# Forgetting attention's outputs as products of split parts, and a new order of the vector work in the long convolution

## The reference

```python
def forgetting_attention(q, k, v, log_f):      # first block, 8 heads of 64
    ...
        logits = jnp.einsum('bqhd,bkhd->bhqk', qi, k).astype(jnp.float32) * scale
        logits = logits + jnp.transpose(Fi, (0, 2, 1))[..., None] - Fk
        mask = pi[:, None] >= kpos[None, :]
        logits = jnp.where(mask, logits, -jnp.inf)
        w = jax.nn.softmax(logits, axis=-1)
        return jnp.einsum('bhqk,bkhd->bqhd', w.astype(v.dtype), v)

def long_conv(u, k_spec, bias):                # second block, called twice
    L = u.shape[1]
    uf = u.astype(jnp.float32)
    y = jnp.fft.irfft(jnp.fft.rfft(uf, n=2 * L, axis=1) * k_spec[None], n=2 * L, axis=1)[:, :L]
    return (y + uf * bias.astype(jnp.float32)).astype(u.dtype)
```

## Time and profile before

| what | value |
|---|---|
| runs | 1761.53 us median of 3 (1761.25 to 1762.07) |
| the profiled execution's own time | 1761.41 us |
| its span, first to last instruction | 1759.6 us |
| mean granted TensorE clock | 0.999 of full speed |
| PE busy | 1734.5 us (99%) |
| DVE busy | 1038.3 us (59%) |
| ACT busy | 632.1 us (36%) |
| POOL busy | 716.0 us (41%) |

### The profile page before, as it was taken

The page is one execution under the profiler, slowest core; times in us unless marked ns, Lnnn a source line. Parts: engine busy times, 40 slices in busy tenths (PEclk is TensorE's granted clock), DMA queues, the critical chain, the costliest instruction groups (busy, mean ns, idle before and its releaser), DMA issues.

```text
span 1759.6 us, 21355 instructions
## 1 busy us (share of the span) xinstructions
PE 1734.5 (99%) x7750; PEld 1400.3 (80%) x7750; DVE 1038.3 (59%) x1185; ACT 632.1 (36%) x876; POOL 716.0 (41%) x299
## 2 busy tenths in 40 slices
PE   8999999999999999999999999999999999999999
PEld 6887788888788888888788788887877777787887
DVE  6767367766654356457674557785534753958541
ACT  5222222225554656221322222213445644333321
POOL 2443344444422421344344344444355434444443
PEclk9999999999999999999999999999999999999999
DMA  4333233324211221243323233322342014232243
GB/s 171 109 105 102 75 99 101 110 90 168 84 61 59 85 72 37 73 133 99 123 96 111 81 101 100 102 96 90 117 150 72 25 37 167 84 101 92 96 137 114
DMA packets 44830, 172.61 MB, mean 98 GB/s; under 512 B 5033, under 2 KB 5161, under 8 KB 43980
## 3 DMA queue, kind: packets, MB, share of 16 engines
q1 hardware_dynamic: 39312, 150.23, 26.0%
q10 hardware_dynamic: 5436, 21.20, 3.4%
HBM read 160.79 MB, written 10.62 MB: 97 GB/s over the span
## 4 chain that ended last, share of the span: by engine, by line
issue 64%; POOL 17%; PE 16%; POOLq 1%; DVE 1%; ACT 1%; DMA 0%; SPq 0%; DVEq 0%; ACTq 0%
POOL wlo L263 17%; PE psum L297 5%; PE psum L299 4%; PE psum L298 4%; PE psum L1598 1%; PE psum L1587 1%; POOLq L271 0%; DMA raw<-wk_dram 0%; PE psum L1559 0%; ACT whi L285 0%; PE psum L1550 0%; POOLq L261 0%; DVE merged_hi L1277 0%; PE psum L1489 0%; DVE sum L1275 0%
## 5 line engine op out<-in xcount | busy, mean ns | idle before, releaser
L263 POOL TENSOR_TENSOR wlo<-raw,whi 128x1024 fp32r<-128x1024 f32 (+2 forms) x262 | 674.0, 2573 | 995.8 <-ACT whi L285 995.8
L285 ACT ACTIVATE whi<-raw 128x1024 fp32r<-128x1024 f32 (+2 forms) x263 | 290.3, 1104 | 741.4 <-PE psum L299 735.4
L297 PE MATMUL psum<-h_hi,whi 128*128 128x512 f32 x1360 | 539.2, 396 | 7.1 <-POOL wlo L263 3.9
L299 PE MATMUL psum<-h_hi,wlo 128*128 128x512 f32 x1360 | 530.7, 390 | 0.0
L298 PE MATMUL psum<-h_lo,whi 128*128 128x512 f32 x1360 | 530.3, 390 | 0.0
L297 PEld LDWEIGHTS psum<-h_hi,whi 128*128 128x128 f32 x1360 | 256.1, 188 | 68.4 <-issue 9.6
L298 PEld LDWEIGHTS psum<-h_lo,whi 128*128 128x128 f32 x1360 | 256.0, 188 | 54.6 <-issue 3.1
L299 PEld LDWEIGHTS psum<-h_hi,wlo 128*128 128x128 f32 x1360 | 255.8, 188 | 54.3
L297 PE MATMUL psum<-mid_hi,whi 128*128 128x512 f32 x352 | 138.1, 392 | 0.0
L298 PE MATMUL psum<-mid_lo,whi 128*128 128x512 f32 x352 | 137.0, 389 | 0.0
L299 PE MATMUL psum<-mid_hi,wlo 128*128 128x512 f32 x352 | 137.0, 389 | 0.0
(11 more groups left out here) (353 smaller groups left out, 2413.7 us busy)
## 6 DMA issues: line engine op xcount, KB each, us to landing
raw<-wk_dram SPq DMA_DIRECT2D x224, 512.0 KB, 3.7
raw<-wd_dram SPq DMA_DIRECT2D x32, 704.0 KB, 4.1
raw<-wp_dram SPq DMA_DIRECT2D x8, 640.0 KB, 3.9
spectra_scratch<-spec_out ACTq DMA_DIRECT2D x8, 512.0 KB, 6.9
x_scratch<-xT ACTq DMA_DIRECT2D x2, 2048.0 KB, 7.6
xT<-x_scratch ACTq DMA_DIRECT2D x8, 512.0 KB, 4.6
spec<-spectra_scratch ACTq DMA_DIRECT2D x2, 2048.0 KB, 10.1
xT<-x_dram SPq DMA_DIRECT2D x4, 512.0 KB, 7.9
```

Source lines behind the costliest of these rows:

```text
L263: pool.tensor_tensor(wlo[s][:, 0:w], raw[s][:, 0:w], whi[s][:, 0:w].bitcast(F32), ALU.subtract).then_inc(lo_ready, 1)
L285: act.activation(whi[s][:, 0:w], raw[s][:, 0:w], ACT.Copy).then_inc(hi_ready, 1)
L297: pe.matmul(dst, s_hi, m_hi, start=start and i == 0, stop=False, **kw)
L299: last = pe.matmul(dst, s_lo, m_hi, start=False, stop=stop and i == n - 1, **kw)
```

## The change

**Forgetting attention.** The values are kept as pairs `v_pairs`: for each head 128 columns, the 64 of one part and the 64 of the other (hi and lo; which comes first depends on the head's parity). The turned probabilities are split as well (`probT_hi` by ACT, `probT_lo` by DVE, `vector_turned`). `tensor_out` is now two fp32r products per tile, both with the same 128 columns of `v_pairs`, one with `probT_hi` and one with `probT_lo`. The 128 output rows hold the hi part's sum in the head's own rows and the lo part's sum in the other 64. ACT copies the other rows across to `ya_shift`, and POOL adds them to `ya_lo` (`pool_outputs`). The sign of the maximum is taken in the reduction itself (`negate=True`), so the instruction of line 778 goes. `vector_norm` and the copies are put in a new order.

**Long convolution.** In the second half the `vector_part` moves ahead of the sums (`low`), the 8 products and 4 sums are written as product, product, sum, and `x2z` moves from behind `vector_z` to the middle of the next products (j = 0) or behind the last `vector_part` (j = 1).

```diff
+        ya_shift = at(24, "ya_shift", [P, 4, T])
-        v32 = at(88, "v32", [P, TT, T])
+        v_pairs = [at(88, "v_pairs0", [P, 2, 2 * T], F32R),
+                   nc.alloc_sbuf_tensor_at("v_pairs1", [P, 2, 2 * T], F32R, offset=scratch0)]
...
             def tensor_turn(self, pe, h, s):
...
                 if n >= 2:
-                    pe.wait_ge((self.copied0, self.copied1)[s % 2], n // 2)
+                    pe.wait_ge(self.lo, n - 1)
...
             def tensor_out(self, pe, h, s):
-                pe.wait_ge((self.copied0, self.copied1)[s % 2], 2 * h + s // 2 + 1)
+                pe.wait_ge(self.lo, TT * h + s + 1)
                 if s == 0:
                     if h:
                         pe.wait_ge(self.out, h)
+                        pe.wait_ge(self.out_hi, 2 * h)
...
-                pe.matmul(psum[:, 512 * 6 + s * P:512 * 7], v32[:, s, (h // 2) * P:(h // 2 + 1) * P],
-                          probT[s % 2][:, s * P:T], start=s == 0, stop=s == TT - 1).then_inc(self.summed, 1)
+                both = v_pairs[s // 2][:, s % 2, h * P:(h + 1) * P]
+                for i, part in enumerate((probT_hi, probT_lo)):
+                    last = pe.matmul(psum[:, 512 * 6 + s * P:512 * 7], both, part[s % 2][:, s * P:T],
+                                     start=s == 0 and i == 0, stop=s == TT - 1 and i == 1)
+                last.then_inc(self.summed, 1)
...
             def scalar_outputs(self, act, h):
-                for s in range(TT):
-                    self.copy_transpose(act, h, s)
-                    if s and h + 1 < HEADS:
-                        self.scalar_exp(act, h + 1, s - 1)
...
+                self.copy_transpose(act, h, 0)
+                self.copy_transpose(act, h, 1)
                 if h + 1 < HEADS:
-                    self.scalar_exp(act, h + 1, TT - 1)
+                    for t in range(TT):
+                        self.scalar_exp(act, h + 1, t)
+                else:
+                    split_hi_to(act, BASE["sb_q"] + 3)
+                self.copy_transpose(act, h, 2)
+                self.copy_transpose(act, h, 3)
...
                 act.activation(ya_hi[rows, h // 2, :], bank(6)[rows, :], ACT.Copy).then_inc(self.out_hi, 1)
+                if h >= 4:
+                    act.wait_ge(self.ready, h - 3)
+                act.activation(ya_shift[rows, h % 4, :], bank(6)[other[h % 2], :],
+                               ACT.Copy).then_inc(self.out_hi, 1)
...
+            def vector_turned(self, dve, h, s):
+                n = TT * h + s
+                dve.wait_ge((self.copied0, self.copied1)[s % 2], n // 2 + 1)
+                src = psum[:, 512 * (4 + s % 2) + s * P:512 * (5 + s % 2)]
+                dve.tensor_tensor(probT_lo[s % 2][:, s * P:T], src, probT_hi[s % 2][:, s * P:T].bitcast(F32),
+                                  ALU.subtract).then_inc(self.lo, 1)
...
+            def pool_outputs(self, pool, h):
+                rows = main[h % 2]
+                pool.wait_ge(self.out_hi, 2 * h + 2)
+                pool.wait_ge(self.out, h + 1)
+                pool.tensor_tensor(ya_lo[rows, h // 2, :], ya_lo[rows, h // 2, :].bitcast(F32),
+                                   ya_shift[rows, h % 4, :], ALU.add).then_inc(self.ready, 1)
...
-                for t, b in ((1, 6), (2, 4), (3, 5)):
-                    act.activation(v32[:, t, :], bank(b), ACT.Copy).then_inc(self.v, 1)
+                act.wait_ge(self.ready, 32)
+                for t, b in ((0, 7), (2, 4), (3, 5), (1, 6)):
+                    act.activation(self.value_part(t, 0), self.heads(bank(b)), ACT.Copy).then_inc(self.v, 1)
...
+                    if j:
+                        merge2.vector_part(dve, 2 * o, 4 * o + 2)
                     for i in range(2):
                         dve.tensor_tensor(low[i][:, :], high[i][:, :], bank(b + 2 * i + 1), ALU.add).then_inc(self.halves, 1)
...
+                        for i in range(2):
+                            self.vector_products(dve, k_low, low, lower, 2 * i, 2 * i + 2)
+                            self.vector_sums(dve, lower, 8 * n, i, i + 1)
+                        hyena_in.vector_x2z(dve, n - 1)
...
+                        for i in range(2):
+                            self.vector_products(dve, k_high, high, upper, 2 * i, 2 * i + 2)
+                            self.vector_sums(dve, upper, 8 * n + 4, i, i + 1)
...
                 merge2.vector_part(dve, 2 * o + 1, self.forth(1))
+                hyena_in.vector_x2z(dve, 2 * o + 1)
```

More of the change, by code:

```diff
@@ L158, in build @@
         probT = [at(104 + 2 * i, f"probT{i}", [P, T]) for i in range(2)]
+        probT_hi = [at(104 + 2 * i, f"probT_hi{i}", [P, T], F32R) for i in range(2)]
+        probT_lo = [nc.alloc_sbuf_tensor_at(f"probT_lo{i}", [P, T], F32R, offset=scratch0 + (8 + 2 * i) * 1024)
+                    for i in range(2)]
         sq_hi = at(32, "sq_hi", [P, HEADS, T], F32R)
@@ L728, in scalar_exp @@
             def scalar_exp(self, act, h, t):
[L729 to L732 removed]
+                if t == 0 and h >= 2:
+                    act.wait_ge(self.turned, TT * (h - 1))
+                act.wait_ge(self.maxed, TT * h + t + 1)
                 n = (t + 1) * P
@@ L794, in vector, with vector_norm @@
                         self.vector_maximum(dve, h + 1)
-                self.vector_outputs(dve, HEADS - 1)
+                    self.vector_turned(dve, h, 0)
+                    self.vector_turned(dve, h, 1)
+                    if h + 1 < HEADS:
+                        self.vector_norm(dve, h + 1)
+                    self.vector_turned(dve, h, 2)
+                    self.vector_turned(dve, h, 3)
+                self.vector_outputs(dve, HEADS - 1)
+            def vector_norm(self, dve, h):
+                total, inverse = self.cols(h, 1), self.cols(h, 2)
+                dve.wait_ge(self.exped, TT * (h + 1))
+                dve.reciprocal(inverse, total).then_inc(self.inv, 1)
+                dve.wait_ge(self.inv, h + 1)
+                for t in range(TT):
+                    row = self.prob[h % 2][:, t, 0:(t + 1) * P]
+                    dve.tensor_scalar(row, row, inverse[:, t:t + 1], None, ALU.mult).then_inc(self.normed, 1)
@@ new lines, in pool @@
+            def pool(self, pool):
+                u = BASE["gate1"] + 3
+                for h in range(HEADS - 1):
+                    pool.wait_ge(lo_ready, u + h)
+                    self.pool_outputs(pool, h)
+                    pool.wait_ge(self.ready, h + 1)
+                    stream_lo(pool, u + h, u + h + 1)
+                stream_lo(pool, u + 7, u + 9)
+                pool.wait_ge(lo_ready, u + 9)
+                self.pool_outputs(pool, HEADS - 1)
+                pool.wait_ge(self.ready, HEADS)
@@ L944, in vector, with vector_values, heads, value_part @@
                 dve.wait_ge(unit_done, BASE["fox_v"] + 4)
-                dve.tensor_copy(v32[:, 0, :], bank(7)).then_inc(merge1.seven_read, 1)
+                self.vector_values(dve, 0, 1)
+            def vector_values(self, dve, first, last):
+                for i, (t, b) in list(enumerate(((0, 7), (2, 4), (3, 5), (1, 6))))[first:last]:
+                    dve.wait_ge(self.v, i + 1)
+                    dve.tensor_tensor(self.value_part(t, 1), self.heads(bank(b)), self.value_part(t, 0).bitcast(F32),
+                                      ALU.subtract).then_inc(merge1.seven_read if b == 7 else self.cleared, 1)
+            def heads(self, b):
+                return b.rearrange("p (a e c) -> p a e c", e=2, c=HD)
+            def value_part(self, t, lo):
+                v = v_pairs[t // 2][:, t % 2, :].rearrange("p (a e c) -> p a e c", e=4, c=HD)
+                return v[:, :, 1:3, :] if lo else v[:, :, 0:4:3, :]
             def vector_logits(self, dve):
@@ L1326, in tensor_part @@
                 else:
-                    pe.wait_ge(fox.out, HEADS)
+                    pe.wait_ge(fox.ready, HEADS)
                     pe.wait_ge(self.seven_read, 10 + b)
@@ L2302, in build @@
         class LongConvolution:
-            signals = [sem(f"long_{x}") for x in ("even", "halves", "products", "upper_products", "spectrum", "f32",
+            signals = [sem(f"long_{x}") for x in ("even", "halves", "products", "spectrum", "f32",
                                                   "hi", "ready", "back", "gated", "gated_hi", "out")]
@@ L2317, in __init__ @@
                 self.o = o
-                (self.even, self.halves, self.prod, self.upper_prod, self.y, self.f32, self.hi, self.ready, self.back,
+                (self.even, self.halves, self.prod, self.y, self.f32, self.hi, self.ready, self.back,
                  self.out32, self.out_hi, self.out) = LongConvolution.signals
```

87 lines of the change are left out of this document (42 added, 45 removed).

## The result

| what | before | after |
|---|---|---|
| median of the runs | 1761.6 us (1761.25 to 1762.07, 4 runs) | 1747.47 us (1746.88 to 1747.85, 4 runs) |
| ratio, 95% interval | | 0.992, 0.9909 to 0.9932 |
| span of the profiled execution | 1759.6 us | 1745.0 us |

The change saves 14.1 us, 0.8%.

The account below looks back on a forecast made before the run. PE, busy 1734.5 of 1759.6 us, was taken to bound the kernel. Output products 6.0, less 0.15 behind the last head, plus long convolutions 3.1 made 9.0 us saved: 1752.5 us, range 1750.8 to 1756.8.

Parts of the forecast that it names:

- output products: Forgetting attention: two fp32r products replace each float32 one, net 0.75 us less a head, 6.0 us for 8 heads.
- long convolution: Second half: PE's wait for `vector_part` goes and its wait for POOL's low part shrinks, 3.1 us for two convolutions.
- POOL gets in at a pause of DVE: Long convolution: POOL's low part enters only when DVE pauses, forecast behind the third pause; 1.57 us saved for both waits.
- My upper bound: Output products: 0.81 us less a head, 6.5 us in all, if no switch of format costs anything.
- Work beside PE: Forgetting attention: work added on ACT, DVE and POOL stays hidden behind PE's filler halves, costed at nothing.
- Rivals C and D: C: late `probT_lo` chain, 1757 to 1759 us, chance 0.08; D: POOL holds DVE ahead of scalings, up to 1773 us, 0.04.
- Behind the last head: After forgetting attention: ACT's extra copy delays POOL's low part, 0.15 us lost, bounds 0 and 0.7.
- rival A: Long convolutions: POOL gets in at once, a gain of 4.0 us there, 1751.6 us in all, chance 0.13.
- `x2z` of the second half: Long convolution: it would stand for most of POOL's 2.40 us low part, outputs about 3 us late, nothing lost for PE.
- Rival B: Long convolutions: POOL stands as long as now, the wait only moves, no gain there, 1755.7 us, chance 0.13.

Follow-up runs that it names:

- Experiment 2: Two edits of the kernel before, on the feed-forward layer's gain: `e5_pool_behind_mid_lo`, 1759.54 us, and `e7_before_padded`, 1758.82 us.
- e13_early_pause: `e1_fox_only` with the fifth product of the long convolution's second half waiting for the fourth, a pause of 0.1 us: 1750.20 us, ratio 0.9934.
- e3_part_moved_only: `e1_fox_only` with `vector_part` moved ahead of the `low` sums, products, sums and `x2z` in the old order: 1747.17 us, ratio 0.9921.
- e1_fox_only: The changed kernel with the long convolution's vector work put back in the old order, so forgetting attention's edit alone: 1752.43 us, ratio 0.9949.
- e7_before_padded: The kernel before with 28 tiny memsets on DVE behind the last output of forgetting attention: 1758.82 us, ratio 0.9984.
- e15_two_more_products: `e1_fox_only` with two more products ahead of the sums in the second half of each long convolution: 1756.89 us, ratio 0.9970.
- e5_pool_behind_mid_lo: The kernel before with POOL's low part of unit 127 waiting until DVE's `mid_lo` in the second feed-forward layer is done: 1759.54 us, ratio 0.9988.

## Why the prediction was wrong, point by point

Three steps failed: the feed-forward layer was left out (2.7 us), the output products were mis-sized (6.0 us for 7.3), and the long convolution was priced by a rule, POOL gets in at a pause of DVE, that is too strict (3.1 us for 4.6).

**What bounds the kernel.** Right: work off PE counted by itself, and all else mattered only where PE waited.

**Output products (-6.0 forecast, -7.3 found).** The mechanism was right, and the term was mis-sized by 0.18 us a head. Out 0 gave 0.40 as forecast (0.86 to 506.93 - 506.47 = 0.46). Out 1 with its step between formats gave 0.21 as forecast (0.67 to 0.46; the 0.26 from 507.07 to 507.33 shows the 0.09). What I left out is the other side of that step: the two transposes between out 0 and out 1 take 0.14 (506.93 to 507.07) where they took 0.22. Outs 2 and 3 gave 0.17 (0.57 to 0.40) instead of 0.14, and scores and filler together 0.07. My upper bound, 6.5 us, assumed that no step could get cheaper.

**Work beside PE.** Right, all of it at nothing: counted from the head's first score (501.22), the first two `probT_lo` were done at +4.2 (forecast 4.4), PE wanted them at +5.3; the exponentials ended at +5.4 (6.0), the scalings at +6.9 (7.5), the last `probT_lo` at +7.5 (8.2). POOL's low part ended at +5.4 (5.3), 0.2 us ahead of the scalings. Rivals C and D did not come. **Behind the last head** 0.2 us were lost against 0.15.

**The feed-forward layer (nothing forecast, -2.7 found).** This step was missing altogether, so that it stood in the sum at nothing, without a reason. The waits of PE in the kernel before named it, 2.1 us in one place; the prediction passed over it and looked only at the stages that the change touches. Experiment 2 shows that 28 more instructions of DVE ahead of it are enough to win it. What stops DVE for 0.35 us is not shown. That it hangs on the place in DVE's stream is, as far as one padding can show it: the work around that place was the same, and PE's weight loads between the first 15 us and it kept their distance from those of the kernel before to 0.1 us. That it was luck for the change is shown with it.

**Long convolution (-3.1 forecast, -4.6 found).** The step that failed is "POOL gets in at a pause of DVE". I read it from one row in which POOL stood through four sums. In the first convolution after the change POOL did get in at a pause, but at the second pause and not, as forecast, at the third: its request came 3.20 us behind the first product, where 3.40 had been placed, just ahead of that pause and not behind it (rival A's "it misses one by 0.2 us"). In the second convolution it missed the pause and was let in 0.33 us later, without one. The experiments show a different rule: POOL is let in behind the instruction of DVE that runs as it asks, pause or not, when DVE has made few instructions since its last pause, and only at a pause when it has made many. POOL got in behind the fourth (`e13_early_pause`) and the eighth (`e3_part_moved_only`, counted from the first difference, ahead of which DVE pauses), and did not behind the twelfth (the kernel before, `e1_fox_only` and its variants). Where between eight and twelve the limit lies was not tried. Nor was it told apart whether all instructions count or only those that read two tiles in SBUF (the sixth product in `e3_part_moved_only`, the eighth in `e1_fox_only`), or whether it is the time since the pause and not the number (POOL asked 1.9 and 4.4 us behind it where it got in, 6.8 us where it did not). With that, rival A's mechanism was the right one, POOL let in at once, and so was its sign, an instruction of POOL of about 2.5 us (2.39 and 2.73). Its 4.0 us were too small as well, by about 0.14 us a wait. Most of that is a cost of the step behind the wait: in the kernel before the product that had waited at 1538.72 was followed in 0.34 us and not in 0.23, and I had counted only the step ahead of it.
The Trainium skill (SBUF — State Buffer, section Who interferes with whom) says that whoever issues first gets the shared pair for its whole instruction. The prediction took it that the loser then waits for one instruction, which the section does not say. The 0.35 and 0.50 us of the short runs agree with that reading; the 2.7 and 3.9 us of the long ones do not, and the measurement decides.
My expectation that `x2z` of the second half would stand 2 us did not come: it asked together with POOL and won. Rival B did not come.

**The sum.** -7.3 + 0.2 - 2.7 - 4.6 = -14.4 us of the 14.6 of span. Of this 11.7 us belong to the change's two ideas, and one of its three edits in the convolution, `vector_part` ahead of the sums, is enough for its part. With the feed-forward layer left out, the time would have been some 1750 us, just below my range, because two terms erred to the same side.

## What to carry to other kernels

Look at every wait of PE in the profile, also far from the change: a collision of DVE and POOL that is decided by less than 0.2 us can flip with any edit that adds instructions ahead of it, and a few idle instructions in the old kernel tell such a gain from one that the change earned. In these runs, where DVE and POOL held each other up over SBUF, a long run of DVE's instructions without a pause made POOL stand through all that was left of it and not through one instruction; a pause of 0.1 us in it, or two of its instructions moved ahead of an earlier pause, was enough against that. When a step between two kinds of work is priced, price it in both directions, for a change can make one of them dearer and the other cheaper (0.09 and 0.08 us here).

## What the runs showed of the hardware

- DVE's stream has places at which an instruction starts 0.35 us late with its semaphore long there (849.87 in the kernel before). With 28 instructions more ahead of it the stop is gone there and stands elsewhere (`e7_before_padded`, and the changed kernel at the same two instructions).
- POOL's entry between DVE's instructions depends on how many of them ran without a pause (or for how long, which was not told apart): let in within 0.5 us behind four (`e13_early_pause`) and eight (`e3_part_moved_only`), kept out for 2.7 us (four more instructions, `e1_fox_only`) and 3.9 us (six more, `e15_two_more_products`) behind twelve.
- In the profiled executions a wait of PE of 2.06 us (before), 2.14 and 2.04 us (`e15_two_more_products`) was followed by some 3.4 us at half the granted clock (products 0.43 us apart); waits of 0.88 and 1.44 us (after) and 1.59 us (`e5_pool_behind_mid_lo`) were not.
- An ordinary float32 product of 512 columns costs 0.86 us of PE (507.42 to 508.28 before), two fp32r products 0.46 (506.47 to 506.93 after).
